# Where the weight tiles lie in SBUF, relative to the activations they are multiplied with

## The reference, cut to what matters

```python
def swiglu(x, w_in, w_out):
    a, b = jnp.split(x @ w_in, 2, axis=-1)
    return (jax.nn.silu(a) * b) @ w_out

for l in range(DEPTH):                      # first block; D_MODEL 1024, D_FF 2816
    x = x + 0.5 * swiglu(rmsnorm(x, ffn1_norm[l]), w_ffn1_in[l], w_ffn1_out[l])
    u = rmsnorm(x, mix_norm[l])
    ...                                     # latent attention, gated recurrence, memory attention
    x = x + merged @ w_out[l]
    x = x + 0.5 * swiglu(rmsnorm(x, ffn2_norm[l]), w_ffn2_in[l], w_ffn2_out[l])
for l in range(DEPTH):                      # second block: the same frame,
    ...                                     # the mixing part is RWKV-7 and retention
```

## Time and profile before

| what | value |
|---|---|
| runs | 2473.41, 2478.52, 2479.93 us; median 2478.52 |
| profiled execution | 2470.84 us, of which 2469.0 us from the first to the last instruction |
| mean granted TensorE clock | 0.996 |
| TensorE matmul busy | 2440.9 us, 99% of the span, 20,948 matmuls |
| TensorE weight load busy | 2380.7 us, 96% |
| VectorE, ScalarE, GpSimd busy | 1673.3, 1279.0, 404.8 us |
| read from HBM | 405.89 MB |

### The profile page before, as it was taken

The page is one execution under the profiler, slowest core; times in us unless marked ns, Lnnn a source line. Parts: engine busy times, 40 slices in busy tenths (PEclk is TensorE's granted clock), DMA queues, the critical chain, the costliest instruction groups (busy, mean ns, idle before and its releaser), DMA issues.

```text
span 2469.0 us, 49272 instructions
## 1 busy us (share of the span) xinstructions
PE 2440.9 (99%) x20948; PEld 2380.7 (96%) x20948; DVE 1673.3 (68%) x2315; ACT 1279.0 (52%) x1812; POOL 404.8 (16%) x357
## 2 busy tenths in 40 slices
PE   8999999999999999999999999999999999999998
PEld 8999999999999999999999999989999999999998
DVE  7765776866667657878666766866666665866664
ACT  5544656644445456565454544745444444754443
POOL 4012110300200210203003013512002003422001
PEclk9999999999999999999999999999999999999999
DMA  6555433455555544345555555403555555402553
GB/s 241 188 188 180 162 124 133 173 188 186 188 188 188 188 171 154 120 139 195 185 190 191 205 203 183 155 19 120 186 185 179 187 189 186 161 26 98 193 188 120
DMA packets 57675, 410.11 MB, mean 166 GB/s; under 512 B 6384, under 2 KB 6640, under 8 KB 8688
## 3 DMA queue, kind: packets, MB, share of 16 engines
q1 hardware_dynamic: 56592, 402.15, 45.9%
q10 hardware_dynamic: 864, 4.82, 0.5%
HBM read 405.89 MB, written 1.05 MB: 165 GB/s over the span
## 4 chain that ended last, share of the span: by engine, by line
PE 87%; DVE 5%; ACT 3%; issue 3%; POOL 2%; DMA 0%; DVEq 0%; SPq 0%; POOLq 0%; ACTq 0%
PE bank L297 86%; DVE sb_wlo L310 2%; ACT area L306 2%; DVE area L310 2%; DVE area L321 1%; PE bank L301 1%; ACT sb_whi L306 1%; POOL area L310 0%; ACT L306 0%; POOL sb_x_ssq L310 0%; POOL area L315 0%; POOL sb_x_sq L310 0%; DVE sb_x L321 0%; DMA sb_x<-x 0%; POOL area L334 0%
## 5 line engine op out<-in xcount | busy, mean ns | idle before, releaser
L297 PE MATMUL bank<-area,sb_whi 128*128 128x256 f32 x11752 | 2093.6, 281 | 11.0 <-DVE area L321 5.7
L297 PEld LDWEIGHTS bank<-area,sb_whi 128*128 128x128 f32 x11752 | 1799.7, 188 | 23.8 <-DVE area L321 9.6
L297 PE MATMUL bank<-area,sb_wlo 128*128 128x256 f32 x5876 | 1642.3, 279 | 4.5 <-DVE sb_wlo L310 4.4
L306 ACT ACTIVATE sb_whi<-sb_raw 128x1024 fp32r<-128x1024 f32 x762 | 801.9, 1058 | 777.0 <-PE bank L297 771.0
L297 PEld LDWEIGHTS bank<-area,sb_wlo 128*128 128x128 f32 x5876 | 1103.6, 188 | 6.4 <-DVE sb_wlo L310 6.4
L310 DVE TENSOR_TENSOR sb_wlo<-sb_raw,sb_whi 128x1024 fp32r<-128x1024 f32 x762 | 962.0, 1271 | 163.2 <-ACT sb_whi L306 161.8
L310 DVE TENSOR_TENSOR area<-area,area 128x256 f32<-128x256 f32 (+7 forms) x502 | 259.7, 526 | 248.4 <-ACT area L306 245.7
L306 ACT ACTIVATE area<-area 128x256 f32<-128x256 f32 (+6 forms) x515 | 252.1, 498 | 83.9 <-DVE area L310 59.1
L310 DVE TENSOR_TENSOR area<-bank,sb_x_diag 128x512 f32<-128x512 f32 x244 | 167.3, 686 | 36.2 <-PE bank L297 21.6
L297 PE MATMUL bank<-area,area 128*64 128x64 f32 (+5 forms) x2304 | 181.4, 254 | 2.1 <-ACT area L306 1.9
L310 POOL TENSOR_TENSOR sb_x_ssq<-sb_x 128x256 f32<-128x256 f32 x12 | 13.1, 1088 | 1014.9 <-DVE sb_x L321 883.0
(11 more groups left out here) (82 smaller groups left out, 705.7 us busy)
## 6 DMA issues: line engine op xcount, KB each, us to landing
sb_raw<-stream SPq DMA_DIRECT2D x379, 1024.0 KB, 4.8
sb_raw<-stream SPq DMA_DIRECT2D x4, 512.0 KB, 6.9
area<-lora ACTq DMA_DIRECT2D x2, 768.0 KB, 4.5
area<-c ACTq DMA_DIRECT2D x1, 1504.0 KB, 7.2
sb_x<-x SPq DMA_DIRECT2D x4, 256.0 KB, 5.0
area<-mem ACTq DMA_DIRECT2D x1, 1024.0 KB, 8.2
out<-sb_x SPq DMA_DIRECT2D x4, 256.0 KB, 2.9
area<-m ACTq DMA_DIRECT2D x1, 512.0 KB, 5.8
```

Of the source, the lines that this page charges most:

```text
L297: return lambda e: e.matmul(out, lhsT, rhs, start=start, stop=stop, skip_group_check=True, tile_position=at)
L306: return lambda e: e.activation(out, a, f, **kw)
```

## The change

The weight slots and the raw buffers get addresses of their own. The arena is moved down to a multiple of 1024 bytes (89,088, residue 0). The slots lie below it in the order `whi0`, `wlo0`, `whi1`, `wlo1` and so on, each 64 bytes below a multiple of 1024, at residue 448. Slot 0 of `whi` and of `wlo` is made of two halves of four blocks: its first half lies at residue 0 and, 448 bytes after its end, its second half at residue 448. So seven blocks of every eight lie 64 bytes below the residue of the moving operands, and one of eight lies at the same residue. All four slots are seen as tensors of shape 128 x 2 x 512, so the two splitting instructions write two runs of 512 elements; in slots 1 to 3 the runs touch. The runtime's reserve for DMA descriptors shrinks from 16,384 to 1,024 bytes. No instruction is added, removed or moved in its queue.

```diff
+ROW = 4 * T
+LINE = 64
+STEP = (512 - LINE) // 4
...
+def place(k, end):
+    k.arena = (end - 4 * ARENA) // ROW * ROW
+    at, k.split_at = k.arena, {}
+    for i in range(SPLIT_SLOTS):
+        for part in range(2):
+            at -= 4 * PIECE * 128
+            k.split_at[part, i] = at - LINE
+            if i == 0:
+                at -= ROW
+                k.split_at[part, i] = at
+    at -= LINE
+    k.raw_at = []
+    for i in range(RAW_SLOTS):
+        at -= 4 * CHUNK_BLOCKS * 128
+        k.raw_at.append(at // 32 * 32)
+    return k.raw_at[-1]
+
+def halves(nc, name, at, step):
+    n = PIECE * 64
+    return nc.alloc_sbuf_tensor_at(name, [128, 2, n + step], F32R, offset=at)[:, :, 0:n]
...
-    w.raw = [sbuf(k, f"raw{i}", [128, CHUNK_BLOCKS * 128]) for i in range(RAW_SLOTS)]
-    w.hi = [sbuf(k, f"whi{i}", [128, PIECE * 128], F32R) for i in range(SPLIT_SLOTS)]
-    w.lo = [sbuf(k, f"wlo{i}", [128, PIECE * 128], F32R) for i in range(SPLIT_SLOTS)]
+    nc, chunk = k.nc, [128, CHUNK_BLOCKS * 128]
+    w.hi, w.lo = ([halves(nc, f"sb_{name}{i}", k.split_at[part, i], STEP if i == 0 else 0)
+                   for i in range(SPLIT_SLOTS)] for part, name in enumerate(("whi", "wlo")))
+    w.raw = [nc.alloc_sbuf_tensor_at(f"sb_raw{i}", chunk, F32, offset=k.raw_at[i]) for i in range(RAW_SLOTS)]
...
-    c = slice(128 * b, 128 * (b + n))
-    return p, w.hi[p % SPLIT_SLOTS][:, c], w.lo[p % SPLIT_SLOTS][:, c], b == 0, b + n == PIECE
+    h, at = divmod(128 * b, PIECE * 64)
+    c = slice(at, at + 128 * n)
+    return p, w.hi[p % SPLIT_SLOTS][:, h, c], w.lo[p % SPLIT_SLOTS][:, h, c], b == 0, b + n == PIECE
...
-        ctx.enter_context(nc.sbuf_tensor("arena", [128, ARENA], F32, side="right"))
-        k.arena, k.placed = nc.sbuf_usable_end // 32 * 32 - 4 * ARENA, 0
+        k.placed = 0
+        low = place(k, nc.sbuf_usable_end // 32 * 32)
+        ctx.enter_context(nc.sbuf_tensor("placed", [128, (nc.sbuf_usable_end - low) // 32 * 8], F32, side="right"))
...
-    nc = bacc.Bacc("TRN2", target_bir_lowering=False, num_devices=1)
+    nc = bacc.Bacc("TRN2", target_bir_lowering=False, num_devices=1, dynamic_dma_scratch_size=1024)
```

More of the change, by code:

```diff
@@ L481, in raw_piece @@
     c, part = divmod(n, PER_CHUNK)
-    return k.w.raw[c % RAW_SLOTS][:, part * PIECE * 128:(part + 1) * PIECE * 128]
+    return k.w.raw[c % RAW_SLOTS][:, part * PIECE * 128:(part + 1) * PIECE * 128].rearrange("p (h n) -> p h n", h=2)
 def split_hi(k, n):
@@ L489, in split_hi @@
         k.act.wait(k.pe, w.used[n - SPLIT_SLOTS])
-    w.hi_done[n] = k.act.mark(activation(w.hi[n % SPLIT_SLOTS][:, :], raw_piece(k, n), ACT.Copy))
+    w.hi_done[n] = k.act.mark(activation(w.hi[n % SPLIT_SLOTS], raw_piece(k, n), ACT.Copy))
 def split_lo(k, n):
@@ L498, in split_lo @@
     s = n % SPLIT_SLOTS
-    w.lo_done[n] = k.dve.mark(remainder(w.lo[s][:, :], raw_piece(k, n), w.hi[s][:, :]))
+    w.lo_done[n] = k.dve.mark(remainder(w.lo[s], raw_piece(k, n), w.hi[s]))
     if n % PER_CHUNK == PER_CHUNK - 1:
```

## The result

The changed kernel runs in 2437.53 us (median of 4 runs, 2436.68 to 2438.49), the kernel before in 2479.22 (4 runs, 2473.41 to 2480.99). The ratio is 0.9839 with a 95% interval of 0.9824 to 0.9854: 1.6% faster, a gain of some 42 us, where 88 were forecast (2390 beside the median of 2478.5 of the runs known then). The time is above the forecast's own range of 2375 to 2414. It is nearest to rival C, the latch (2438). The profiled execution took 2437.49 us, 2435.7 of it from the first to the last instruction, 33.3 less than the profiled one before, which had been faster than all four runs of its kernel.

A forecast was written before the change was run, and what follows sets the result against it. TensorE was taken as the bound: number of matmuls times their pace. Gains of 80.2, 1.8 and 5.1 us, times 0.93, gave 81 us off 2470.8, so 2390 us; range 2340 to 2478, the forecast's own 2375 to 2414.

The forecast's parts named there:

- rival C: Weight matmuls: the latch stays, pace 117.7 or 113.3 ns by the last disturbance; half the time fast, 2438 us; chance 0.15.
- I read this as two streams that meet: TensorE's weight matmuls: moving-operand and next-weight reads meet in memory once per period; their interleaving sets paces 4.4 ns apart.
- seven blocks of eight at 64 bytes below: Weight slots: seven eighths of the slow matmuls go from 117.7 to 112 ns, gaining 80.2 us.
- The floor: Weight matmuls: pace without the meeting, taken as 112 ns, between 110 from other rows and the fast latch's 113.3.
- the two terms: Seven of eight weight blocks at 112 ns: 80.2 us from the slow matmuls and 1.8 us from the fast.
- One block of eight at the same residue: First half of slot 0: pace 115 ns, gaining 5.1 us; it might throw the stream into either pace.
- What reaches the end: Whole kernel: all feed-forward matmuls and three quarters of those in mixing parts count, so 0.93 of the gain.
- The latch and the spread of the runs: Weight matmuls: the fast pace, once entered after an interruption, stays; 1,545 fast matmuls, 6.8 us, explain the runs' spread.
- D: Weight matmuls: paces come from TensorE's own clocking, not addresses, so no effect, 2471 to 2479 us; chance 0.12.
- E: Weight matmuls: nearly equal residues make both streams start together, pace 122.1 ns, slower by 84 us, 2555 us; chance 0.13.
- The parts costed at nothing: Splits in two runs, smaller descriptor reserve, moved addresses and the 128x512 products: no effect counted on the time.

The follow-up runs named there:

- e1: Changed kernel with no block at the same residue, all weights 64 bytes below the moving operands: 2479.39 us, ratio 1.0012 to the kernel before.
- e2: Changed kernel with slots 320 bytes below, the old distance, keeping the first half of slot 0 at the same residue: 2438.23 us, ratio 0.9842.
- e4: Changed kernel with every weight slot at the residue of the moving operands: 2512.0 us in one run.
- e12: Changed kernel with slot 0 wholly 64 bytes below in the steady stretches of feed-forward parts: 2426.61 us, ratio 0.9821 to the kernel before.
- e3: Changed kernel with slots 320 bytes below everywhere, the old distance, and no block at the same residue: 2477.14 us in one run.
- e11: The changed kernel repeated unaltered on another chip: 2437.27 us (5 runs), ratio 0.9847 to the kernel before.

## Why the prediction was wrong

**"I read this as two streams that meet", and the distance.** This is the step that failed. The sum's first and largest term, 80.2 us for "seven blocks of eight at 64 bytes below", supposes that the new distance is free of meetings and so faster. By itself it is worth nothing: e1 has it everywhere, at 117.7 ns and 2479.39 us beside 2477.84, and e2 has the whole gain without it. The seven eighths did get faster, by the passages between them. That addresses act on the pace holds: with addresses alone changed it goes to 120 (e4). That two reads meet is not shown. In every run with weights at the residue of the moving operands both lie at residue 0, so it may be the weights' own address that counts. No run has both at an equal residue other than 0, which would tell.

**The floor, "between these I take 112".** This is the second error, of size. The rows at 110 to 112 were of another float format and showed no pace that this stream can take: in none of the twelve experiments is the steady fast pace below 113.3. The row nearest in operation was the fast latch itself, which the prediction named and then went below. With 113.3 for 112 the two terms are 14,070 x 4.4 = 62 us. But not even all of those matmuls were fast: 3,385 remained at 116 to 119 ns, mostly behind interruptions, until a passage worked. The mean of the seven eighths is 114.24, so the two terms measure 15,250 x (117.32 - 114.24) = 47 us against 82.

The Trainium skill ("TensorE: Matmul & The Clock Gate", "Back-to-back issue gap") gives a gap of N / 2.4 + 2.5 ns, 109.2 for 256 columns, for an isolated matmul, and says that in a stream of weight loads and matmuls both set the spacing. No steady pace of this stream comes nearer to 109.2 than 113.3.

**"One block of eight at the same residue, I take 115."** It costs 119.9 ns in the mean and 120 in the steady state, above the end "no change" of the stated bounds: 2,170 x (117.3 - 119.9) = -5.6 us instead of +5.1. Yet this eighth makes the whole gain, by the sentence that followed its price, that it could throw the stream into the one or the other pace. The prediction took that for a disturbance without a side and gave it no term. It has one: a fast stream stays fast, and a slow one comes out fast in 78 of 106 cases.

**"What reaches the end", 0.93.** Of 41.5 us gained in pace 33.3 reached the end of the profiled execution, 0.80. The feed-forward parts gave nearly all of theirs, 33 of 34.6 us. The mixing parts, of which the prediction counted three quarters, gave practically nothing: 6.7 us in pace, 0.3 us in time (975.0 before, 974.7 after). It came back as longer interruptions (in the whole run 73.2 us in 213 of them over 160 ns, before 63.8 in 189). That TensorE is busy for 97% there doesn't say that it is what the next step waits for.

**The latch and the spread of the runs.** Confirmed in its first half: a fast pace stays if nothing interrupts it (1,428 steps in e12). In the changed kernel 29 interruptions of a fast stream can be followed, and 26 of them left it slow. The second half, that the number of fast matmuls makes the spread, is borne out in part: the profiled execution before had 1,842 of them and e3 822, which at 4.4 ns is 4.5 of the 6.3 us between the two. The changed kernel leaves less of this to chance: its four runs lie within 1.8 us, those before within 7.6. On another chip, though, five runs of it spread over 6.8 (e11), so not all of the spread is this.

**The rivals.** C was right in its mechanism ("the address alone doesn't set the pace"). That its time, 2438, was met to the microsecond is luck: it supposed half of the slow matmuls to be fast and 0.93 to reach the end, where 12,151 of 17,628 were fast, 1,869 went at 120 and 0.80 reached it. It expected windows of 852 and 885 in a mix; there are 878 everywhere in the steady parts, since it lacked the regular return. D ("from TensorE's own clocking, not from addresses") is excluded by e4 for the 120, and by the changed kernel beside e1 for the way into the 113.3. That 64 below and 192 above give the same two paces, though, is what D said. The Trainium skill ("SBUF — State Buffer", "Who interferes with whom") gives TensorE two independent read ports, one for the moving operand and one for LDWEIGHTS, and says that TensorE never waits on anyone. By that, as the prediction read it, all distances would cost the same; here they take 117.7 and 120.0 ns with nothing but the addresses of the weight buffers changed (e3 and e4), and the measurement decides. E's price, a mean above 117.3 from reads at nearly the same residue, is true of exactly the same residue, at 2.3 ns instead of 4.4, and not of 64 bytes below.

**The parts costed at nothing** (splits in two runs, smaller reserve, arena's place, wide products) were right: e3 gives the time of the kernel before.

**What stays open.** Why even steps of 120 lead into the fast pace, where the two paces come from, and whether the 120 belongs to an equal residue or to weights at a multiple of 512 bytes, no run shows. The trace gives starts; it doesn't show reads of SBUF. Nor is it shown why the kernel before has a median of 2478 us on one chip and 2472 on another.

## What to carry to other kernels

When one instruction runs at two paces in one trace, with the same operands and clock, look for a state that it can be latched in before you look for a better constant, and take the pace that was already seen as the bound of what a change can give. A change with two edits in its name needs each undone alone; here the one that looked like a remainder made the gain and the one that looked like the point made none. Before you count a faster engine's gain to the end, compare the same stretch before and after: busy for 97% and on the path are not the same. If a cheap disturbance puts a stream into its good state and the state lasts, put it only behind the places that lose it, as e12 does.

## What the runs showed of the hardware

A stream of float32r matmuls with 256 moving columns and a new load of 128 columns each ran at three steady paces at full clock. With the weights 64 bytes below or 192 above the residue of the moving operand (modulo 512 bytes) it ran at 113.3 or 117.7 ns, both possible at either distance. With both at residue 0 it ran at 120.0 ns and no other. A passage of twelve at the same residue left every fast stream fast and turned a slow one fast in 78 of 106 cases (changed kernel, e2, e11, e12), always after it had come to even steps of 120 ns; a passage of six did it in 23 of 45. Without a passage the slow pace prevailed (e1: 17,125 of 17,628 at 116 to 119 ns). That a deliberate stretch at the slowest pace makes the whole faster was not expected.
